# Another order of attention scores, gate blocks and transposes in a two-layer transformer mixer on one core

## The chip, the cores and the metric

The kernel runs on one core of one Trainium2 chip. The metric is the device time of one launch in microseconds (us); less is better. Before the change three runs gave 2495.41, 2496.18 and 2497.45 us, so the median is 2496.18 us.

## The reference, cut to what matters

The program computes a first block (a gated mixer of two branches and a mixture of 16 experts) and then a second block of two layers. Everything that is changed lies in the mixer of those two layers, `token_mixer_2`, on 256 tokens of width 1024:

```python
proj = u @ w_in                      # q 512, k 128, v 128, p 512, gates 2 x 1024
q, k = partial_rope(q), partial_rope(k)
scores = where(|qpos - kpos| <= 128, q @ k.T / 8, -1e30)      # 8 heads
probs = softmax(concat([scores, sink]))[..., :-1]
y_attn = (probs @ v) @ w_br_attn
y_pool = multiscale_pool(p) @ w_br_pool
out = (sigmoid(ga + b) * y_attn + sigmoid(gb + b) * y_pool) @ w_out
```

Each of the two layers is: half a feed-forward, this mixer, half a feed-forward, each on a normalized input and added to the stream.

## The kernel before, in words

Weights come as a stream of slots of 128x2048 fp32 values, 1 MB each, through a ring of 8 slots. SyncE reloads a slot when TensorE has signalled that it is used (`slot_used`, line 302). In the two layers every weight is taken apart into two fp32r numbers: ScalarE rounds a slot into `w_hi` (three buffers; `upper(n)`, line 499) and VectorE subtracts it from the slot in place (`lower(n)`, line 954). TensorE then makes three products for one (`product3`, line 1494). `upper(n)` waits until slot n-3 is used, for its buffer.

Each engine runs its own written list of steps and meets the others at semaphores alone. Nothing reorders the steps of ScalarE or VectorE: whatever stands at the head of the list holds back all behind it. The steps of one layer's mixer, with the names that matter here:

- **Gate blocks.** `gate(k)`, k from 0 to 7, is 48 matmuls on TensorE into bank 6 + k % 2 (line 1558); ScalarE's `gate(k)` waits for it, makes two sigmoids into `sgate` (line 551, tile mixer_area in the trace) and then does `upper` of the slot three further on (line 554). TensorE's gate(k) waits for ScalarE's gate(k-2), since they share a bank. TensorE's gate(k) also waits for VectorE's `lower` of slot 5 + k of the mixer.
- **Turned q and k.** Ten transposes (lines 1567 to 1571) into banks 0 to 2, copied out by ScalarE (lines 559 to 561, `qkT_kept`).
- **Scores.** `scores(t)` for the two halves of the queries, t = 0 and 1. TensorE makes eight small matmuls into banks 0 to 3. VectorE scales and masks them out of the banks (line 1020, `scores_kept`), takes the maximum (line 1024) and three small steps (`max_ready`). ScalarE's `exponentials(t)` makes eight exponentials with sums and one small one (lines 567 and 569, `att_exp`). VectorE's `probabilities(t)` scales by one over the sum (lines 1033 to 1035, `att_ready`). scores(1) on TensorE waits for `scores_kept` of half 0, since the banks are the same.
- **Transposes of probabilities.** `turn_att(c)`, c from 0 to 7, is four transposes; c from 0 to 3 is half 0, c from 4 to 7 half 1 (line 1582). Even c go to bank 4 and are copied by VectorE (line 1041), odd c go to bank 5 and are copied by ScalarE (line 574). turn_att(2) waits for VectorE's copy of 0, turn_att(3) for ScalarE's copy of 1.
- **Behind them.** Pooling matmuls (line 1608), mixed (line 1614), attention times v (line 1624), branch projections and the output projection.

The tiles have other names in the trace: `att` is area_h, `attT` is area_n, `sgate` and the maxima are mixer_area. TensorE's matmuls all have line 1101, its transposes line 1110.

The lists before, as far as they are touched. TensorE: gate 0, gate 1, turns of q and k, gate 2, scores 0, gate 3, gate 4, scores 1, turn_att 0, turn_att 1, gate 5, turn_att 2, turn_att 3, pooling, gate 6, mixed, gate 7, turn_att 4 to 7. ScalarE: gate 0, gate 1, copies of q and k, gate 2, exponentials 0, gate 3, gate 4, copy 1, exponentials 1, gate 5, copy 3, pooled copy, and so on. VectorE: lower 7, 8, 9, scores 0, lower 10, probabilities 0, lower 11, scores 1, lower 12, copy 0, copy 2, lower 13, probabilities 1, lower 14.

Of the kernel before, what the change touches and what calls it, by code (L numbers as in the profile page):

```python
# [25 lines left out]
TT = T // P  # L26
# [42 lines left out]
MIX_AT = 33  # L69
# [50 lines left out]
def build(nc, d):  # L120

    with ExitStack() as ctx:
# [5 lines left out]
        def sig(name):  # L128
            if name not in signals:
                signals[name] = ctx.enter_context(nc.semaphore(name))  # L130
            return signals[name]
# [44 lines left out]
        def bank(i):  # L176
            return ps[:, i, :]
# [4 lines left out]
        def lcol(name, i=0, n=1):  # L182
            return lcols[:, LCOLS[name] + i:LCOLS[name] + i + n]
# [128 lines left out]
        def _(act):  # L312
# [168 lines left out]
            with act.Fori(0, LAYERS) as l:  # L481
# [10 lines left out]
                def upper(n):  # L492

                    turn = l * (LAYER_SLOTS // RING) + (first + n) // RING
                    act.wait_ge(sig(f"slot_loaded{n % RING}"), turn * 16 + 16)
                    if n >= SPLITS:

                        act.wait_ge(sig("slot_used"), l * LAYER_SLOTS + first + n + 1 - SPLITS)
                    A.copy(w_hi[:, n % SPLITS, :], ring[:, n % RING, :]).then_inc(sig("w_hi_ready"), 1)  # L499
# [48 lines left out]
                def gate(k):  # L548
                    act.wait_ge(sig("gate_ps"), l * KD + k + 1)
                    for g in range(2):  # L550
                        last = A.activation(sgate[:, k, g, :], bank(6 + k % 2)[:, g * T:(g + 1) * T], ACT.Sigmoid,
                                            bias=lcol("b_gates", 8 * g + k))
                    last.then_inc(sig("gate_kept"), 1)
                    upper(MIX_AT + 8 + k)

                for k in range(2):
                    gate(k)
                act.wait_ge(sig("qkT_ps"), l + 1)
                A.copy(q2T[:, 0:2, :], bank(0).rearrange("p (j t) -> p j t", j=2))
                A.copy(q2T[:, 2:4, :], bank(1).rearrange("p (j t) -> p j t", j=2))  # L560
# [2 lines left out]
                def exponentials(t):  # L563

                    act.wait_ge(sig("max_ready"), l * TT + t + 1)
                    for h in range(8):
                        A.activation(att[:, t, h, :], att[:, t, h, :], ACT.Exp, bias=mst[:, t, 2, h:h + 1],  # L567
                                     accum_out=mst[:, t, 3, h:h + 1])
                    A.activation(mst[:, t, 1, :], mst[:, t, 1, :], ACT.Exp).then_inc(sig("att_exp"), 1)

                def keep_att(c):

                    act.wait_ge(sig("attT_ps"), l * 8 + c + 1)
                    A.copy(attT[:, (c // 2) % 2, (c % 2) * 4:(c % 2) * 4 + 4, (c // 4) * P:(c // 4 + 1) * P],
                           bank(4 + c % 2).rearrange("p (h q) -> p h q", h=4)).then_inc(sig("attT_kept_a"), 1)

                gate(2)
                exponentials(0)
                gate(3)
                gate(4)  # L580
                keep_att(1)
                exponentials(1)
                gate(5)
                keep_att(3)
                act.wait_ge(sig("pooled_ps"), l + 1)
                A.copy(pooledT, ps[:, 2:4, :].rearrange("p b (j t) -> p (b j) t", j=2)).then_inc(sig("pooled_kept"), 1)
                gate(6)
# [23 lines left out]
        def _(dve):  # L611
# [167 lines left out]
            for h in range(H):  # L779
# [28 lines left out]
                n = inter.rearrange("p t (s e) -> p t s e", s=2)[:, :, :, P]  # L808
# [136 lines left out]
            with dve.Fori(0, LAYERS) as l:  # L945
# [5 lines left out]
                def lower(n):  # L951

                    dve.wait_ge(sig("w_hi_ready"), l * SPLIT_SLOTS + n + 1)
                    V.tensor_tensor(ring_lo[:, n % RING, :], ring[:, n % RING, :], w_hi[:, n % SPLITS, :].bitcast(F32),  # L954
                                    ALU.subtract).then_inc(sig("w_ready"), 1)
# [59 lines left out]
                def scores(t):  # L1015

                    dve.wait_ge(sig("scores_ps"), l * TT + t + 1)
                    a = att[:, t, :, :]
                    m = mst[:, t, 0, :]
                    V.scalar_tensor_tensor(a, ps[:, 0:4, :].rearrange("p b (f k) -> p (b f) k", f=2), 0.125,  # L1020
                                           amask[:, t, :].unsqueeze(1).broadcast_to([P, 8, T]),
                                           ALU.mult, ALU.add).then_inc(sig("scores_kept"), 1)
                    dve.wait_ge(sig("scores_kept"), l * TT + t + 1)
                    step(V.tensor_reduce(m, a, X, ALU.max))  # L1024
                    step(V.tensor_tensor(m, m, lcol("sink", 0, 8), ALU.max))
                    V.tensor_tensor(mst[:, t, 1, :], lcol("sink", 0, 8), m, ALU.subtract)
                    V.tensor_scalar(mst[:, t, 2, :], m, -1.0, None, ALU.mult).then_inc(sig("max_ready"), 1)

                def probabilities(t):
                    dve.wait_ge(sig("att_exp"), l * TT + t + 1)  # L1030
                    a = att[:, t, :, :]
                    m = mst[:, t, 0, :]
                    step(V.tensor_tensor(m, mst[:, t, 3, :], mst[:, t, 1, :], ALU.add))
                    step(V.reciprocal(m, m))
                    V.tensor_tensor(a, a, m.unsqueeze(2).broadcast_to([P, 8, T]),
                                    ALU.mult).then_inc(sig("att_ready"), 1)

                def keep_att(c):

                    dve.wait_ge(sig("attT_ps"), l * 8 + c + 1)  # L1040
                    V.tensor_copy(attT[:, (c // 2) % 2, 0:4, (c // 4) * P:(c // 4 + 1) * P],
                                  bank(4).rearrange("p (h q) -> p h q", h=4)).then_inc(sig("attT_kept"), 1)

                for n in range(MIX_AT + 7, MIX_AT + 10):
                    lower(n)
                scores(0)
                lower(MIX_AT + 10)
                probabilities(0)
                lower(MIX_AT + 11)
                scores(1)  # L1050
                lower(MIX_AT + 12)
                keep_att(0)
                keep_att(2)
                lower(MIX_AT + 13)
                probabilities(1)
                lower(MIX_AT + 14)
                for g in range(4):
                    if g == 0:
# [35 lines left out]
        def _(pe):  # L1094
# [206 lines left out]
            for o in range(ORDERS):  # L1301
# [30 lines left out]
                for j in range(4):  # L1332
                    n = 0
# [90 lines left out]
            with pe.Fori(0, NE) as e:  # L1424
# [21 lines left out]
                for i in range(8):  # L1446
                    w = slot(2 * KD + i, turns)
                    for c in range(2):
                        for j in range(2):
                            k = 2 * i + j  # L1450
# [18 lines left out]
            with pe.Fori(0, LAYERS) as l:  # L1469
# [9 lines left out]
                def split(n):  # L1479

                    pe.wait_ge(sig("w_ready"), l * SPLIT_SLOTS + n + 1)
                    return w_hi[:, n % SPLITS, :], ring_lo[:, n % RING, :]
# [75 lines left out]
                def gate(k):  # L1558
                    if k >= 2:
                        pe.wait_ge(sig("gate_kept"), l * KD + k - 1)  # L1560
                    pair(split(MIX_AT + 5 + k), bank(6 + k % 2), sig("gate_ps"))

                for k in range(2):
                    gate(k)
                pe.wait_ge(sig("rope_ready"), l + 1)
                pe.wait_ge(sig("vp_kept"), l + 1)
                for j in range(5):
                    for t in range(TT):
                        turn(bank(j // 2)[:, (j % 2) * T + t * P:(j % 2) * T + (t + 1) * P],
                             qk[:, t, 2 * j:2 * j + 2, :].rearrange("p h c -> p (h c)"),  # L1570
                             ready=sig("qkT_ps") if j == 4 and t == 1 else None)
                gate(2)
                pe.wait_ge(sig("qkT_kept"), l + 1)

                def scores(t):
                    for j in range(4):
                        for f in range(2):

                            mm(bank(2 * f + j // 2)[:, (j % 2) * T:(j % 2 + 1) * T], q2T[64 * f:64 * f + 64, j, t * P:(t + 1) * P],
                               k2T[64 * f:64 * f + 64, :], ready=sig("scores_ps") if j == 3 and f == 1 else None)  # L1580

                def turn_att(c):

                    t, k, half = c // 4, (c // 2) % 2, c % 2
                    pe.wait_ge(sig("att_ready"), l * TT + t + 1)
                    if c >= 2:

                        pe.wait_ge(sig("attT_kept") if c % 2 == 0 else sig("attT_kept_a"), l * 4 + c // 2)
                    for i in range(4):
                        turn(bank(4 + c % 2)[:, i * P:(i + 1) * P], att[:, t, half * 4 + i, k * P:(k + 1) * P],  # L1590
                             ready=sig("attT_ps") if i == 3 else None)


                scores(0)
                gate(3)
                gate(4)
                pe.wait_ge(sig("scores_kept"), l * TT + 1)
                scores(1)
                turn_att(0)
                turn_att(1)  # L1600
                gate(5)
                turn_att(2)
                turn_att(3)

                pe.wait_ge(sig("scores_kept"), l * TT + 2)
                for g in range(4):
# [35 lines left out]
                for i in range(KD // 2):  # L1642
                    w = split(MIX_AT + 17 + i)
                    pe.wait_ge(sig("mT_ready"), l * KD + 2 * i + 2)
                    for t in range(TT):
                        for j in range(2):
                            k = 2 * i + j
# [176 lines left out]
```

## Time and profile before

| | |
|---|---|
| runs | 2495.41, 2496.18, 2497.45 us |
| profiled execution, its own time | 2499.19 us |
| span of its profile | 2497.3 us |
| TensorE busy | 2158.2 us (86%) |
| VectorE busy | 823.1 us (33%) |
| ScalarE busy | 597.7 us (24%) |
| granted TensorE clock, mean over the span | 0.919 |
| HBM read | 655.97 MB, 263 GB/s over the span |

The span is the time from the first to the last instruction in the profile; the run's own time is 1.9 us longer. The two layers take the last 1100 us of the span; the first layer's mixer begins near 1596 us, the second's near 2145 us. The granted clock is given as a share of 2.4 GHz: 1.00 is 2.4 GHz and 0.50 is 1.2 GHz. A stretch with a value between them holds a change from one to the other.

### The profile page before, as it was taken

How to read it: one execution, taken by the hardware profiler on the slowest of the kernel's cores; microseconds unless marked ns; L12 is line 12 of the kernel's file. 1: busy time of each engine (PE TensorE's matmuls, PEld its weight loads, DVE VectorE, ACT ScalarE, POOL GpSimd, SP SyncE). 2: the span in 40 equal slices, each digit the busy share in tenths (PEclk: the TensorE clock that was granted, in tenths of full speed). 3: DMA queues.
4: the chain of work that ended last, by engine and by line, in shares of the span. 5: the costliest groups of instructions: out<-in, count | busy, mean ns of one | idle time of the engine just before them, and what ended most of it. 6: DMA issues, size and time to landing. Idle time of an engine off the chain costs nothing.

```text
span 2497.3 us, 31333 instructions
## 1 busy us (share of the span) xinstructions
PE 2158.2 (86%) x12642; PEld 1440.0 (58%) x12642; DVE 823.1 (33%) x1079; ACT 597.7 (24%) x715; POOL 0.2 (0%) x4
## 2 busy tenths in 40 slices
PE   7999898777777777777777799998999999999998
PEld 2477674222222222222222699897999899888998
DVE  3422533000000000000000555556555555556554
ACT  2311101000000000000000433463433433463333
POOL 0000000000000000000000000000000000000000
PEclk9999998988788878888878899999999999999999
DMA  8336433999999999999999555433455455433552
GB/s 341 114 119 231 172 118 127 409 422 422 422 422 422 422 422 422 422 422 422 422 422 421 224 185 186 167 134 139 169 186 186 175 186 186 169 119 135 186 187 92
DMA packets 91395, 658.49 MB, mean 264 GB/s; under 512 B 10144, under 2 KB 10528, under 8 KB 11808
## 3 DMA queue, kind: packets, MB, share of 16 engines
q1 hardware_dynamic: 88992, 647.01, 65.8%
q10 hardware_dynamic: 2304, 10.05, 1.1%
q8 instruction: 76, 1.25, 0.2%
q14 instruction: 23, 0.19, 0.0%
HBM read 655.97 MB, written 1.05 MB: 263 GB/s over the span
## 4 chain that ended last, share of the span: by engine, by line
PE 62%; DMA 27%; DVE 5%; ACT 3%; issue 2%; SPq 0%; ACTq 0%; DVEq 0%
PE ps L1101 61%; DMA ring<-stream_dram 26%; PE ps L1110 1%; ACT w_hi L499 1%; ACT later L477 1%; DVE later L924 0%; DVE area_h L1020 0%; DVE mixer_area L1024 0%; DMA wide<-filt_dram 0%; DVE later L918 0%; DVE later L914 0%; DVE wide L788 0%; ACT area_h L567 0%; DVE wide L795 0%; DVE area_n L622 0%
## 5 line engine op out<-in xcount | busy, mean ns | idle before, releaser
L1101 PE MATMUL ps<-ring,later 128*32 128x512 f32 x3072 | 581.8, 750 | 208.4 <-DMA ring<-stream_dram 177.1
L1101 PEld LDWEIGHTS ps<-ring,later 128*32 128x32 f32 x3072 | 112.7, 124 | 648.0 <-DMA ring<-stream_dram 448.5
L954 DVE TENSOR_TENSOR ring_lo<-ring,w_hi 128x2048 fp32r<-128x2048 f32 x174 | 398.7, 2292 | 246.4 <-ACT w_hi L499 245.7
L1101 PE MATMUL ps<-u_hi,w_hi 128*128 128x256 f32 x1664 | 474.4, 285 | 2.9 <-DVE u_lo L961 2.9
L1101 PE MATMUL ps<-u_lo,w_hi 128*128 128x256 f32 x1664 | 473.0, 284 | 0.0
L1101 PE MATMUL ps<-u_hi,ring_lo 128*128 128x256 f32 x1664 | 472.1, 284 | 0.0
L499 ACT CAST w_hi<-ring 128x2048 fp32r<-128x2048 f32 x174 | 331.1, 1904 | 219.9 <-PE ps L1101 219.8
L1101 PEld LDWEIGHTS ps<-u_hi,w_hi 128*128 128x128 f32 x1664 | 318.8, 192 | 7.8 <-DVE u_lo L961 5.6
L1101 PEld LDWEIGHTS ps<-u_lo,w_hi 128*128 128x128 f32 x1664 | 317.6, 191 | 1.7
L1101 PEld LDWEIGHTS ps<-u_hi,ring_lo 128*128 128x128 f32 x1664 | 318.2, 191 | 0.0
L477 ACT COPY later<-ps 128x1024 f32<-128x1024 f32 x16 | 16.2, 1012 | 636.6 <-PE ps L1101 636.6
L924 DVE TENSOR_TENSOR later<-later,ps 128x512 f32<-128x512 f32 x16 | 11.0, 689 | 474.8 <-PE ps L1101 474.8
L1101 PE MATMUL ps<-area_h,ring 128*128 128x256 f32 (+1 forms) x640 | 153.4, 401 | 1.8 <-DVE wide L828 1.8
L1101 PEld LDWEIGHTS ps<-area_h,ring 128*128 128x128 f32 x640 | 121.4, 190 | 33.5 <-issue 17.1
L914 DVE TENSOR_TENSOR later<-ps,mod 128x256 f32<-128x256 f32 x16 | 6.8, 425 | 401.2 <-PE ps L1101 401.2
L1101 PE MATMUL ps<-w_hi,hid_lo 128*128 128x512 f32 x352 | 139.0, 395 | 0.0
L1101 PE MATMUL ps<-w_hi,hid_hi 128*128 128x512 f32 x352 | 138.5, 393 | 0.0
L1101 PE MATMUL ps<-ring_lo,hid_hi 128*128 128x512 f32 x352 | 138.0, 392 | 0.0
L524 ACT ACTIVATE area_n<-ps 128x256 f32<-128x256 f32 x88 | 33.8, 385 | 314.4 <-PE ps L1101 314.4
L1101 PE MATMUL ps<-wide 128*128 128x130 f32 (+5 forms) x244 | 73.6, 458 | 25.1 <-DMA wide<-filt_dram 8.7
L982 DVE TENSOR_TENSOR hid_hi<-ps,area_n 128x256 fp32r<-128x256 f32 x88 | 37.4, 425 | 154.7 <-ACT area_n L524 154.7
L1101 PE MATMUL ps<-later 128*128 128x512 f32 x144 | 68.3, 619 | 17.8 <-ACT later L477 17.8
(245 smaller groups left out, 1816.9 us busy)
## 6 DMA issues: line engine op xcount, KB each, us to landing
ring<-stream_dram SPq DMA_DIRECT2D x616, 1024.0 KB, 14.6
wide<-filt_dram ACTq DMA_DIRECT2D x1, 1728.0 KB, 7.5
wide<-tabs_dram ACTq DMA_DIRECT2D x1, 1408.0 KB, 10.4
tabs<-tabs_dram ACTq DMA_DIRECT2D x1, 1296.0 KB, 5.8
x_tok<-x_dram ACTq DMA_DIRECT2D x1, 1024.0 KB, 14.6
area_n<-ctx_dram ACTq DMA_DIRECT2D x1, 1024.0 KB, 19.1
fin_rows<-fin_rows_dram ACTq DMA_DIRECT2D x2, 512.0 KB, 4.2
out_dram<-x_tok SPq DMA_DIRECT2D x2, 512.0 KB, 2.6
```

What stands on the lines that cost most here:

```text
L477: A.copy(ye, ps[:, 6:8, :].rearrange("p b n -> p (b n)")).then_inc(sig("ye_ready"), 1)
L499: A.copy(w_hi[:, n % SPLITS, :], ring[:, n % RING, :]).then_inc(sig("w_hi_ready"), 1)
L524: A.activation(sa2[:, i % 2, :], bank(4 + i % 4)[:, 0:T], ACT.Silu).then_inc(sig("silu2_ready"), 1)
L914: V.tensor_tensor(xe, bank(5)[:, 0:KD * CAP].rearrange("p (k c) -> p k c", k=KD), mod2[:, :].unsqueeze(2).broadcast_to([P, KD, CAP]), ALU. ...
L924: V.tensor_tensor(hid_e, sa, bank(5), ALU.mult).then_inc(sig("hid_e_ready"), 1)
L954: V.tensor_tensor(ring_lo[:, n % RING, :], ring[:, n % RING, :], w_hi[:, n % SPLITS, :].bitcast(F32), ALU.subtract).then_inc(sig("w_ready" ...
L982: V.tensor_tensor(hid_hi[:, i % 4, :], b, sa2[:, i % 2, :], ALU.mult)
L1101: ins = M.matmul(out, lhsT, rhs, start=start, stop=stop, **more)
L1110: ins = M.transpose(out, src, ident[0:rows, 0:rows])
```

## The change

It only moves steps within the written lists of ScalarE, VectorE and TensorE, in the body of the loop over the two layers. No instruction is added or taken away, and no semaphore's meaning changes. After it, TensorE's list is: gate 0, turns of q and k, gate 1, scores 0, gate 2, scores 1, gate 3, gate 4, turn_att 0 to 3, gate 5, pooling, gate 6, mixed, gate 7, turn_att 4 to 7. ScalarE's is: gate 0, copies of q and k, gate 1, exponentials 0, gate 2, gate 3, exponentials 1, gate 4, copy 1, copy 3, gate 5, pooled copy. VectorE's is: lower 7, 8, scores 0, lower 9, scores 1, probabilities 0, lower 10, 11, copy 0, copy 2, probabilities 1, lower 12, 13, 14.

```diff
--- before.py
+++ after.py
@@ -553,8 +553,7 @@
                     last.then_inc(sig("gate_kept"), 1)
                     upper(MIX_AT + 8 + k)
 
-                for k in range(2):
-                    gate(k)
+                gate(0)
                 act.wait_ge(sig("qkT_ps"), l + 1)
                 A.copy(q2T[:, 0:2, :], bank(0).rearrange("p (j t) -> p j t", j=2))
                 A.copy(q2T[:, 2:4, :], bank(1).rearrange("p (j t) -> p j t", j=2))
@@ -574,14 +573,15 @@
                     A.copy(attT[:, (c // 2) % 2, (c % 2) * 4:(c % 2) * 4 + 4, (c // 4) * P:(c // 4 + 1) * P],
                            bank(4 + c % 2).rearrange("p (h q) -> p h q", h=4)).then_inc(sig("attT_kept_a"), 1)
 
+                gate(1)
+                exponentials(0)
                 gate(2)
-                exponentials(0)
                 gate(3)
+                exponentials(1)
                 gate(4)
                 keep_att(1)
-                exponentials(1)
+                keep_att(3)
                 gate(5)
-                keep_att(3)
                 act.wait_ge(sig("pooled_ps"), l + 1)
                 A.copy(pooledT, ps[:, 2:4, :].rearrange("p b (j t) -> p (b j) t", j=2)).then_inc(sig("pooled_kept"), 1)
                 gate(6)
@@ -1041,18 +1041,19 @@
                     V.tensor_copy(attT[:, (c // 2) % 2, 0:4, (c // 4) * P:(c // 4 + 1) * P],
                                   bank(4).rearrange("p (h q) -> p h q", h=4)).then_inc(sig("attT_kept"), 1)
 
-                for n in range(MIX_AT + 7, MIX_AT + 10):
+                for n in range(MIX_AT + 7, MIX_AT + 9):
                     lower(n)
                 scores(0)
+                lower(MIX_AT + 9)
+                scores(1)
+                probabilities(0)
                 lower(MIX_AT + 10)
-                probabilities(0)
                 lower(MIX_AT + 11)
-                scores(1)
-                lower(MIX_AT + 12)
                 keep_att(0)
                 keep_att(2)
+                probabilities(1)
+                lower(MIX_AT + 12)
                 lower(MIX_AT + 13)
-                probabilities(1)
                 lower(MIX_AT + 14)
                 for g in range(4):
                     if g == 0:
@@ -1560,8 +1561,7 @@
                         pe.wait_ge(sig("gate_kept"), l * KD + k - 1)
                     pair(split(MIX_AT + 5 + k), bank(6 + k % 2), sig("gate_ps"))
 
-                for k in range(2):
-                    gate(k)
+                gate(0)
                 pe.wait_ge(sig("rope_ready"), l + 1)
                 pe.wait_ge(sig("vp_kept"), l + 1)
                 for j in range(5):
@@ -1569,7 +1569,7 @@
                         turn(bank(j // 2)[:, (j % 2) * T + t * P:(j % 2) * T + (t + 1) * P],
                              qk[:, t, 2 * j:2 * j + 2, :].rearrange("p h c -> p (h c)"),
                              ready=sig("qkT_ps") if j == 4 and t == 1 else None)
-                gate(2)
+                gate(1)
                 pe.wait_ge(sig("qkT_kept"), l + 1)
 
                 def scores(t):
@@ -1592,15 +1592,14 @@
 
 
                 scores(0)
+                gate(2)
+                pe.wait_ge(sig("scores_kept"), l * TT + 1)
+                scores(1)
                 gate(3)
                 gate(4)
-                pe.wait_ge(sig("scores_kept"), l * TT + 1)
-                scores(1)
-                turn_att(0)
-                turn_att(1)
+                for c in range(4):
+                    turn_att(c)
                 gate(5)
-                turn_att(2)
-                turn_att(3)
 
                 pe.wait_ge(sig("scores_kept"), l * TT + 2)
                 for g in range(4):
```

## Rows read from the trace of the kernel before

**Rows 1.** The page's chain that ended last, by engine, shares of the span.
```profile
PE 62%; DMA 27%; DVE 5%; ACT 3%; issue 2%; SPq 0%; ACTq 0%; DVEq 0%
```

**Rows 2.** Waits in the first layer's mixer, TensorE and DMA queue: total, times, longest.
```profile
PE ps L1110 <- DVE area_n L1041: 3.5, 2, 3.2
PE ps L1110 <- ACT area_n L574: 1.4, 1, 1.4
...
SPq L303 <- PE ps L1101: 67.4, 9, 14.7
```

**Rows 3.** Timeline of TensorE, first layer's mixer: start, length, instruction, [idle before].
```profile
1624.59 0.28 PE L1101 MATMUL ps<-u_hi,w_hi 128*128 128x256 f32 x1
...
1636.02 1.26 PE L1110 MATMUL ps<-const,hid_area 128*128 128x128 f32 x10
...
1637.03 0.36 PE L1101 MATMUL ps<-u_hi,w_hi 128*128 128x256 f32 x1
...
1642.92 2.00 PE L1101 MATMUL ps<-mixer_area 64*128 64x256 f32 x16
...
1644.85 0.39 PE L1101 MATMUL ps<-u_hi,w_hi 128*128 128x256 f32 x1
...
1656.48 2.00 PE L1101 MATMUL ps<-mixer_area 64*128 64x256 f32 x16
...
1658.41 1.09 PE L1110 MATMUL ps<-const,area_h 128*128 128x128 f32 x8
...
1668.37 1.97 PE L1110 MATMUL ps<-const,area_h 128*128 128x128 f32 x8 [3.16 <-DVE area_n L1041]
```

**Rows 4.** Timeline of ScalarE, the same stretch.
```profile
1643.03 0.84 ACT L551 ACTIVATE mixer_area<-ps,lcols 128x256 f32<-128x256 f32 x2 [2.93 <-PE ps L1101]
...
1643.75 1.90 ACT L499 CAST w_hi<-ring 128x2048 fp32r<-128x2048 f32 x1
...
1645.67 1.28 ACT L567 ACT_TABLE_LOAD   x1
...
1650.09 0.51 ACT L567 ACTIVATE area_h<-area_h,mixer_area 128x256 f32<-128x256 f32 x1 [3.14 <-DVE mixer_area L1027]
...
1658.80 1.92 ACT L499 CAST w_hi<-ring 128x2048 fp32r<-128x2048 f32 x1
...
1660.60 0.61 ACT L574 COPY area_n<-ps 128x512 f32<-128x512 f32 x1
```

**Rows 5.** Timeline of VectorE, the same stretch.
```profile
1644.96 2.29 DVE L1020 SCALAR_TENSOR_TENSOR area_h<-ps,tabs 128x2048 f32<-128x2048 f32 x1 [3.79 <-PE ps L1101]
...
1649.97 2.28 DVE L954 TENSOR_TENSOR ring_lo<-ring,w_hi 128x2048 fp32r<-128x2048 f32 x1
...
1654.28 0.17 DVE L1033 TENSOR_TENSOR mixer_area<-mixer_area 128x8 f32<-128x8 f32 x1 [2.03 <-ACT mixer_area L569]
...
1654.72 2.29 DVE L1035 TENSOR_TENSOR area_h<-area_h,mixer_area 128x2048 f32<-128x2048 f32 x1
...
1667.63 0.69 DVE L1041 COPY area_n<-ps 128x512 f32<-128x512 f32 x1
```

**Rows 6.** Busy us (x) of PE, PEld, DVE, ACT, POOL; PEclk; DMA share; GB/s.
```profile
1668.37:1670.34 1.97, 1.97 (x9) 1.97 (x10) 0.69 (x1) 1.95 (x8) 0.00 (x0) 0.50 0.30 33
...
1670.34:1675.47 5.13, 5.13 (x16) 4.13 (x16) 1.81 (x1) 3.77 (x5) 0.00 (x0) 0.61 0.47 192
...
2217.19:2219.16 1.97, 1.97 (x9) 1.97 (x10) 0.69 (x1) 1.95 (x8) 0.00 (x0) 0.50 0.31 42
...
2219.16:2222.97 3.81, 3.81 (x18) 3.24 (x16) 0.48 (x1) 3.77 (x5) 0.00 (x0) 0.83 0.61 254
...
2241.16:2246.36 5.20, 5.20 (x32) 3.47 (x33) 0.30 (x1) 0.00 (x0) 0.00 (x0) 0.69 0.01 3
```

**Rows 7.** Timeline of TensorE's turns ahead of the first mixer.
```profile
1592.62 3.50 PE L1110 MATMUL ps<-const,area_n 128*128 128x128 f32 x16 [2.63 <-DVE area_n L622]
```

**Rows 8.** Stretch at the end of those turns, columns as in rows 6.
```profile
1595.00:1596.00 1.00, 1.00 (x7) 0.88 (x5) 0.08 (x1) 0.95 (x3) 0.00 (x0) 0.59 0.89 369
```

## The prediction

> **What bounds the kernel now.** I read the page's chain first: TensorE carries 62% of it and the DMA of weights 27% [rows 1]. The DMA share lies in the first block and the experts. In the two layers the DMA queue waits for TensorE to free slots, 67.4 us in nine waits within one mixer [rows 2], so loads are not what a new order there can help or harm. Then I read TensorE's waits in one mixer [rows 2]. Of all its idle time the one large piece is 3.2 us before turn_att(2), ended by VectorE's copy of turn_att(0). The second layer's answer has the same rows. Then the timelines of the three engines over the same stretch [rows 3 to 5]: from 1624.59 on TensorE goes without a gap through gates, turns and scores until gate 5 ends, stands until 1668.37, and goes on. The last view is the granted clock in stretches [rows 6]: after this stall it is at 0.50, that is 1.2 GHz, and what follows runs slowly.
>
> So an order of steps can be worth three things per layer: the 3.2 us stall, the slow running behind it, and any new stall. TensorE's own work is the same before and after, since nothing is added.
>
> **What VectorE was doing in the stall.** Its copy of turn_att(0) stands behind scores(1) and lower 12 and starts at 1667.63 [rows 5]; the transposes for it had been made at about 1659. The change moves scores(1) forward by two gates, so that this copy no longer waits for it. That part does what it says. But turn_att(3) waits for the other copy, ScalarE's, and ScalarE's list has changed too: exponentials(1) and gate 4 now stand before it.
>
> **The working, first layer.** Lengths from the rows: a gate block takes (1636.02 - 1624.59) / 2 = 5.71 us, or (1656.48 - 1644.85) / 2 = 5.82 us behind small work; ten turns 1.01 us (1637.03 - 1636.02); scores 1.93 us (1644.85 - 1642.92) [rows 3].
>
> TensorE after: gate 0 from 1624.59, turns of q and k at 1630.30, gate 1 at 1631.31, scores(0) one gate earlier than now, at 1642.92 - 5.71 = 1637.21, gate 2 at 1639.14, scores(1) at 1644.96, gate 3 at 1646.89, gate 4 at 1652.71. Gate 4 ends at 1658.41, as the same five gates, turns and both scores do now [rows 3].
>
> Do the waits on this way hold it? The turns of q and k end at 1631.3; until scores(0) at 1637.2 ScalarE has one cast (1.9 us) and three copies (0.6 us each, by the copy of the same width) to do, 3.7 us [rows 4]: no wait. VectorE reads scores(0) at 1644.96 - 5.71 = 1639.25 and is done 2.29 later, at 1641.6 [rows 5]; scores(1) wants the banks at 1644.96: no wait, 3.4 us to spare. The maxima are there 5.13 us after that reading starts (1644.96 to 1650.09) [rows 4, 5], so exponentials(0) starts at 1644.38 and lasts 4.19 us (1650.09 to 1654.28), to 1648.57. Then ScalarE loads its table (1.28 us [rows 4]) and makes gate 2's sigmoids, done by 1650.7. Gate 4 wants that bank at 1652.71: no wait, with 2.0 us to spare. VectorE does lower 9 (2.29 us [rows 5]) in between, then scores(1) from 1647.0 to 1652.1, probabilities(0) in 2.73 us (1654.28 to 1654.72 + 2.29) [rows 5] to 1654.8, lower 10 and 11 until 1659.2, and copies turn_att(0) until 1659.9. TensorE made turn_att(0) and (1) by 1659.5, so it waits **0.4 us** for turn_att(2), in place of 3.2.
>
> Now turn_att(3). ScalarE starts gate 3's sigmoids 0.11 us behind TensorE's end of that block [rows 3, 4], at 1652.8. Sigmoids to cast 0.72 us, cast to table load 1.92 us [rows 4]: the table for exponentials(1) is loaded from 1655.5 to 1656.8, 4.7 us after the maxima of half 1 are ready at 1652.1. Exponentials(1) then take 4.19 us, to 1660.9. Gate 4's table load and sigmoids: 1.28 + 0.72, to 1662.9. Its cast: 1.80 us (1658.80 to 1660.60) [rows 4], to 1664.7. The copy of turn_att(1): 0.61 us [rows 4], to 1665.3. Handing over to TensorE takes 0.05 us (1667.63 + 0.69 against 1668.37) [rows 3, 5]. TensorE has ended turn_att(2) at 1660.5 and waits for turn_att(3) until 1665.4: **4.9 us**. Queued behind it are gate 5 and all that follows.
>
> Stalls: 5.3 us in place of 3.2 us, plus 0.1 us because four transposes alone don't overlap those behind them: +2.2 us a layer. Both layers have the same timing, so **+4.5 us**. What else moved costs nothing: lower 12 ends near 1667.2 and gate 7 wants it after 1680, under cover of gates 5 and 6; if that cover went, its 2.29 us would show. The waits behind gate 7 (1.4 us for ScalarE's copy of turn_att(5) [rows 2], and smaller ones) stay, as their lists are unchanged. Bounds of the stall term: VectorE's and ScalarE's parts could each be off by one small operation, some 0.3 us; ends +1.6 and +2.8 us a layer.
>
> **The clock.** Behind the stall the first layer ran eight turns at 0.50 and pooling at 0.61: 1.97 x 0.50 + 5.13 x 0.39 = 3.0 us lost. The second ran them at 0.50 and 0.83: 1.0 + 3.81 x 0.17 = 1.6 us lost; 4.6 in all [rows 6]. With a longer stall the clock is surely low when TensorE resumes, and gate 5 takes the place of turns and pooling as the work that runs slowly. I bound each layer by these two rows, 1.6 and 3.0, and take their mean, 4.6 for both layers. The same program also lost 5.20 x 0.31 = 1.6 us in the second layer behind gate 7 and not in the first [rows 6], so this part varies by itself.
>
> The profiled execution took 2499.19 us, 3.0 above the median. That is just what lies between it and an execution with two short slow stretches (3.2 in place of 4.6 us) and none behind gate 7 (1.6). Against the median the clock term of the change is then between 0 and +1.4; I take +0.6. Sum: 2499.19 + 4.5 for the profiled execution at equal clock, and **2496.18 + 4.5 + 0.6 = 2501.3 us** for the median.
>
> **A rule against the rows.** Eight turns at 0.50 come first behind the stall now; after the change only four, then a block of real matmuls. Ahead of the first mixer sixteen turns alone took 3.50 us [rows 7], and the clock was back near their end (0.59 in a stretch that ends at 1.00, or 1595.8) [rows 8]. The Trainium skill, TensorE: Matmul & The Clock Gate, section Part 4: PE-mode transpose, says that transposes don't count as work that brings the full clock back. The trace disagrees there, as turns alone brought it back. By the page the new order should always give the short stretch: the rival below gives its time from rows.
>
> **Rivals.**
> - The clock returns early in both layers, since matmuls follow the stall almost at once: 1.6 us lost in each, 3.2 in place of 4.6. For: the second layer's 0.83 [rows 6]. Against: rows 7 and 8, and the first layer's stretch with the same instructions. Time: 2496.18 + 4.5 - 1.4 = 2499.3. Chance 0.25; within 0.2%.
> - The clock stays low for the long stretch in both layers: 3.0 each, 6.0 in place of 3.2 for a median execution. 2496.18 + 4.5 + 2.8 = 2503.5. For: the longer stall. Chance 0.22; slower.
> - Faster: turn_att(3) finds its copy made and both stalls vanish, the clock stays up. 2 x 3.2 + 4.6 = 11.0 us less, 2485.2. It decides at ScalarE's start of copy 1, which would have to be by about 1660, while I have exponentials(1) ending at 1660.9 and 3.8 us of gate 4 before the copy. Half of it (exponentials(1) starting at 1652.1) would still give a faster kernel. For: VectorE's chain did get shorter. Against: ScalarE's written order. Chance 0.08.
>
> **How the numbers follow.** My forecast has 0.45 and lies at 2499.9 to 2502.7, on both sides of 0.2% (5.0 us, about what a measurement of this kernel can tell from no change): 0.26 of it above, 0.19 below. Slower: 0.26 + 0.22 = 0.48. Same: 0.19 + 0.25 = 0.44. Faster: 0.08. The range leaves out the faster case: low end 2496.18 + 3.2 - 1.4 = 2498.0 (stall at its lower bound, short slow stretches), high end 2496.18 + 5.6 + 2.8 = 2504.6.
>
> **What would show it.** Right: in both layers a wait of TensorE for area_n of line 574 of 4 to 6 us before a group of four transposes, a wait for line 1041 under 1 us, and PEclk 0.50 at the start of gate 5. exponentials(1) start right behind a table load, not behind a wait for VectorE. Wrong: no wait above 1 us before gate 5; or a new wait before gate 4 or scores(1); or a gain behind gate 7.

## The result and the profile after

The changed kernel takes 2502.89 us in the median of 10 runs (2501.49 to 2506.62), the kernel before 2495.57 us in 10 runs (2494.17 to 2498.33). The ratio is 1.0031, 95% interval 1.0023 to 1.0040: slower by 7.3 us. The forecast was 2501.3 us, with a range of 2498.0 to 2504.6.

The profiled execution of the changed kernel took 2502.87 us at a span of 2501.0 us. The waits of TensorE over both mixers, total, times and longest; line 573 is ScalarE's copy of a turned block, 1041 VectorE's, and TensorE's transposes are now line 1111:

```profile
PE ps L1111 <- DVE area_n L622: 15.5, 7, 4.8
PE ps L1111 <- ACT area_n L573: 13.0, 4, 5.1
...
PE ps L1111 <- DVE area_n L1041: 1.4, 4, 0.3
```

The wait that stood before, 3.2 us for VectorE's copy [rows 2], has shrunk to 0.35 us. In its place is one of 5.1 us for ScalarE's copy, in both layers. The timeline of TensorE in the first layer's mixer shows where:

```profile
1629.79 1.25 PE L1111 MATMUL ps<-const,hid_area 128*128 128x128 f32 x10
...
1636.69 2.00 PE L1102 MATMUL ps<-mixer_area 64*128 64x256 f32 x16
...
1644.52 2.00 PE L1102 MATMUL ps<-mixer_area 64*128 64x256 f32 x16
...
1657.99 1.03 PE L1111 MATMUL ps<-const,area_h 128*128 128x128 f32 x8
1659.37 0.66 PE L1111 MATMUL ps<-const,area_h 128*128 128x128 f32 x4 [0.35 <-DVE area_n L1041]
1665.13 1.09 PE L1111 MATMUL ps<-const,area_h 128*128 128x128 f32 x4 [5.10 <-ACT area_n L573]
```

From the turns of q and k to turn_att(1) nothing waits; the scores of half 1 come 12 us earlier than before (1644.52 against 1656.48 [rows 3]). Then turn_att(3) stands for 5.10 us. ScalarE's timeline says what it did meanwhile:

```profile
1655.12 1.28 ACT L566 ACT_TABLE_LOAD   x1
1656.41 0.51 ACT L566 ACTIVATE area_h<-area_h,mixer_area 128x256 f32<-128x256 f32 x1
...
1660.58 1.28 ACT L551 ACT_TABLE_LOAD   x1
1661.87 0.84 ACT L551 ACTIVATE mixer_area<-ps,lcols 128x256 f32<-128x256 f32 x2
1662.60 1.90 ACT L499 CAST w_hi<-ring 128x2048 fp32r<-128x2048 f32 x1
1664.39 0.59 ACT L573 COPY area_n<-ps 128x512 f32<-128x512 f32 x1
```

Exponentials 1, a table load, gate 4's sigmoids and its cast run one behind another, and the copy comes last. The maxima of half 1 were ready at 1651.6, but exponentials 1 could only start at 1656.41, so the earlier scores brought nothing here: ScalarE was the engine with the queue.

The granted clock (PEclk is the third number from the end) from turn_att(3) to the end of gate 5 in both layers, and through attention times v in the first:

```profile
1665.13:1673.86 8.73, 8.73 (x53) 8.73 (x54) 1.69 (x1) 0.59 (x1) 0.00 (x0) 0.68 0.00 0
2217.61:2225.04 7.43, 7.43 (x52) 7.43 (x53) 1.70 (x1) 0.59 (x1) 0.00 (x0) 0.82 0.00 0
1695.32:1700.32 5.00, 5.00 (x33) 3.36 (x33) 0.30 (x1) 0.00 (x0) 0.00 (x0) 0.72 0.02 3
```

Lost behind the two waits: 8.73 x 0.32 + 7.43 x 0.18 = 4.1 us, and 1.4 us behind gate 7. The profiled execution before lost 4.6 and 1.6 us in these places [rows 6]. So between the two profiled executions the clock in these places counts for -0.7 us, and the stalls for +4.6 us (2 x (0.35 + 5.10 - 3.16)); 3.9 us together, and the two executions lie 3.7 us apart. The medians lie 7.3 us apart, of which the stalls explain 4.6. What the other 2.7 us are is the question that one pair of profiles can't answer.

### The profile page after: what moved, and what is told of

The parts are those of the page before. It is cut to its first block, busy times and chain, and to the rows that moved or that the text cites. A ratio compares the mean times of both kernels' runs of the same rounds, so it can differ in the third digit from the quotient of the medians.

```text
span 2501.0 us, 31333 instructions
## 1 busy us (share of the span) xinstructions
PE 2159.9 (86%) x12642; PEld 1437.9 (57%) x12642; DVE 822.7 (33%) x1079; ACT 598.1 (24%) x715; POOL 0.2 (0%) x4
## 4 chain that ended last, share of the span: by engine, by line
PE 63%; DMA 27%; DVE 5%; ACT 3%; issue 2%; SPq 0%; ACTq 0%; DVEq 0%
PE ps L1102 62%; DMA ring<-stream_dram 26%; PE ps L1111 1%; ACT w_hi L499 1%; ACT later L477 1%; DVE later L924 0%; DMA wide<-filt_dram 0%; DVE later L918 0%; DVE later L914 0%; ACT area_h L566 0%; DVE wide L788 0%; DVE wide L795 0%; DVE area_n L622 0%; ACT area_n L333 0%; ACT wide L433 0%
```

## The experiments

My theory: the stall sits in ScalarE's list, ahead of its copy of turn_att(1), and the rest is the clock. Each ratio below is against runs of the kernel before on the same chip.

**The copy ahead of gate 4.** In ScalarE's list:

```diff
                 exponentials(1)
+                keep_att(1)
                 gate(4)
-                keep_att(1)
                 keep_att(3)
```

> The changed kernel with ScalarE's copy of turn_att(1) put ahead of its gate 4 instead of behind it. My theory (the changed kernel waits 5.1 us per layer for this copy because ScalarE's list has exponentials 1 and gate 4 ahead of it, and the clock falls in that wait): the copy starts behind exponentials 1 near 1660.6 in place of 1664.4, the wait for line 573 shrinks from 5.1 to about 1.3 us in both layers, 7.7 us less, and where the clock stays at 1.00 another 3 to 5 us less: 2490 to 2492 us, some 4 to 5 us under the kernel before. Rival (another thing ends the wait, such as a weight slot or VectorE): the wait stays near 5 us and the time within 2 us of 2502.9.

Measured: 2490.84 us, ratio 0.9979 (0.9969 to 0.9989). TensorE's timeline and the granted clock from turn_att(3) to the end of gate 5 in the first layer:

```profile
1660.06 0.63 PE L1111 MATMUL ps<-const,area_h 128*128 128x128 f32 x4 [1.14 <-ACT area_n L573]
```

```profile
1660.06:1666.24 6.18, 6.18 (x52) 6.18 (x53) 4.51 (x2) 4.27 (x5) 0.00 (x0) 1.00 0.22 91
```

One step moved ahead of one other takes the wait from 5.10 to 1.14 us (1.15 in the second layer), and the clock stays at 1.00 in both layers. The whole gain is 12.0 us, of which 7.9 are the waits. The rival falls.

**Gate 5 back between the transposes.** On TensorE; ScalarE's copy 3 goes behind gate 5 to match:

```diff
-                for c in range(4):
+                for c in range(2):
                     turn_att(c)
                 gate(5)
+                for c in range(2, 4):
+                    turn_att(c)
```

> The changed kernel with gate 5 put back between turn_att(1) and turn_att(2) on TensorE (and between copies 1 and 3 on ScalarE); the new order of scores stays. My theory: gate 5 covers both waits, since copy 1 is made at about 1665.0 and gate 5 ends at 1664.9; no wait over 0.4 us ahead of pooling, 10.9 us less than the changed kernel, and with the clock at 1.00 through the gates another 3 to 5 us: 2487 to 2489 us. Rival (the new order of scores itself costs time, on whichever engine): a new wait of some us elsewhere before gate 6, and a time at or above the kernel before, 2495.6.

Measured: 2485.48 us, ratio 0.9961 (0.9947 to 0.9975), 17.4 us under the changed kernel and 10.6 us under the runs of the kernel before. Timeline and waits of TensorE in the first layer's mixer:

```profile
1657.09 1.04 PE L1111 MATMUL ps<-const,area_h 128*128 128x128 f32 x8
1663.68 1.19 PE L1111 MATMUL ps<-const,area_h 128*128 128x128 f32 x8
```

```profile
PE ps L1111 <- ACT area_n L573: 1.4, 1, 1.4
...
PE ps L1111 <- DVE area_n L1041: 0.3, 1, 0.3
```

No wait is left before pooling; the rows that remain belong behind gate 7. The time is even 1.5 us under what I had written. So the change has two parts of opposite sign. Scores of both halves early, which this version keeps, is a gain of 10.6 us: 6.3 us are the two old waits, and that the other 4.3 us are the clock is argued and not shown. The transposes put together ahead of gate 5 cost 17.4 us. The sum is a loss of 6.8 us, against 7.3 measured.

**The wait filled with matmuls.** To part the clock from the stall, the changed kernel does 40 extra matmuls in its long wait. They read `u_hi` and write bank 0, which is free there. In the run's kernel they stand in a small helper; here, and in the other fillings, they are written out in place:

```diff
-                for c in range(4):
+                for c in range(3):
                     turn_att(c)
+                for i in range(40):
+                    mm(bank(0)[:, 0:T], u_hi[:, i % 8, 0:P], u_hi[:, i % 8, :])
+                turn_att(3)
                 gate(5)
```

> The changed kernel with 40 extra matmuls of 0.12 us, whose product nothing reads, put into TensorE's wait before turn_att(3): the wait's length stays, but the clock has no idle stretch to fall in. If the part of the loss beyond the stalls (7.3 us measured less 4.6 of longer stalls) is the clock: the granted clock is 1.00 through gate 5, and the time is 4 to 5 us less than the changed kernel, about 2498 us. Rival (the clock is not part of it): within 1 us of 2502.9, or above by what the filling overruns.

Measured: 2493.54 us (12 runs, 2490.48 to 2503.19), ratio 0.9991 (0.9979 to 1.0003). That is 9.4 us less with more work, not 4 to 5. The granted clock from the filling to the end of gate 5 in the first layer:

```profile
1657.16:1668.69 11.53, 11.21 (x95) 11.04 (x94) 5.55 (x5) 5.76 (x11) 0.00 (x0) 1.00 0.21 85
```

So the clock behind the wait is part of the loss, and the rival falls. But the gain is over twice the 4.1 us that the changed kernel's profile lost there.

**The same for the kernel before**, with 24 matmuls ahead of turn_att(2), into bank 6 behind a wait for gate 4's sigmoids:

```diff
                 gate(5)
+                pe.wait_ge(sig("gate_kept"), l * KD + 5)
+                for i in range(24):
+                    mm(bank(6)[:, 0:T], u_hi[:, i % 8, 0:P], u_hi[:, i % 8, :])
                 turn_att(2)
```

> The kernel before with 24 extra matmuls of 0.12 us, whose product nothing reads, put into TensorE's 3.2 us wait before turn_att(2). The clock stays at 1.00 through turns and pooling. If the kernel before lost less to the clock than the changed one in the median (my reading: 2 to 3 us in place of 4 to 6), this gains only 2 to 3 us, to about 2493 us, and the difference of the two filled kernels is that of the stalls alone, 4.6 us. Rival (both lose the same to the clock): this gains 4 to 5 us, to 2491, and the filled kernels differ by 7 us.

Measured: 2491.74 us, ratio 0.9983 (0.9974 to 0.9992), 4.3 us under the runs of the kernel before. That is the gain that I wrote for the rival (4 to 5), not that of my reading (2 to 3). The granted clock is 1.00 behind the filled wait:

```profile
1672.22:1676.77 4.55, 4.54 (x26) 4.13 (x27) 0.69 (x1) 4.52 (x11) 0.00 (x0) 1.00 0.28 117
```

The second half of the expectation fails for both: the two filled kernels differ by 1.8 us, where my reading had the 4.6 us of the stalls and the rival 7. Their intervals overlap, but 1.8 us says that filling gave the changed kernel more than the clock behind its two waits, or that scatter of some 2 us is left in these medians (the same filled kernel comes out 2.1 us higher below).

**The changed kernel again, filled and not, on one chip.**

> The changed kernel, unaltered, once more on the chip of the two that follow, so that they can be compared without a change of chip. My theory: 2502 to 2504 us again, two waits for line 573 of 5.1 us, and the granted clock at 0.50 behind each, for 3 to 6 us of busy time.

> The first filled version of the changed kernel once more (40 matmuls whose product nothing reads in the 5.1 us wait). It came out 9.4 us under the changed kernel, more than the 4.3 us that its profile shows lost behind the two waits. Theory A (the clock term is near 6 us in the median and the rest was scatter): 2495 to 2497 us, 6 to 8 us under the unaltered one. Theory B (filling gives more than the clock): 2493 to 2494 again, 9 to 10 us under.

Measured: 2503.57 us without (7 runs, 2501.47 to 2504.26; ratio 1.0028, 1.0017 to 1.0039), 2495.67 us filled (11 runs, 2492.49 to 2503.09; ratio 1.0004, 0.9995 to 1.0013): 7.9 us. Time and difference are those of theory A, the difference at its upper end. The granted clock in the profile of the unfilled one, from turn_att(3) to the end of gate 5 and through attention times v, in each layer:

```profile
1665.15:1673.88 8.73, 8.73 (x52) 8.73 (x53) 1.70 (x1) 0.59 (x1) 0.00 (x0) 0.67 0.00 0
1695.34:1700.40 5.06, 5.06 (x33) 3.43 (x33) 0.30 (x1) 0.00 (x0) 0.00 (x0) 0.72 0.02 3
2217.90:2227.00 9.10, 9.10 (x54) 9.07 (x55) 1.69 (x1) 0.66 (x2) 0.00 (x0) 0.68 0.00 0
2248.19:2253.30 5.11, 5.11 (x33) 3.44 (x33) 0.30 (x1) 0.00 (x0) 0.00 (x0) 0.71 0.01 3
```

and of the filled one, from the filling to the end of gate 5:

```profile
1658.62:1670.15 11.53, 11.21 (x96) 11.03 (x94) 5.55 (x5) 5.76 (x11) 0.00 (x0) 1.00 0.21 85
2205.14:2216.68 11.54, 11.22 (x95) 11.05 (x94) 5.55 (x5) 5.77 (x11) 0.00 (x0) 1.00 0.22 87
```

The same program as in the first profile after lost 2.9 us behind each wait here (8.73 x 0.33, 9.10 x 0.32), and 1.4 and 1.5 us behind gate 7. The filled one lost nothing in these places.

But the two profiled spans, 2501.8 and 2492.4 us, differ by more than their mixers do. From the first transposes of a mixer to those of the feed-forward behind it the filled execution is 3.8 us shorter in the first layer (1592.15 to 1750.84 against 1590.80 to 1745.70) and 2.3 us in the second (2144.88 to 2303.61 against 2135.78 to 2292.24). That is 6.1 us of the 9.4; the other 3.3 us lie where not one instruction differs. One such place is the start of the feed-forward behind the first mixer, where TensorE waits 2.3 to 2.4 us for its input in every version. The clock in the ten microseconds behind that wait, for the kernel before, the same filled, the changed kernel and the same filled:

```profile
1747.95:1757.95 10.00, 9.06 (x50) 8.43 (x51) 6.44 (x11) 6.49 (x13) 0.00 (x0) 0.66 0.27 105
1750.55:1760.55 10.00, 8.44 (x66) 7.93 (x67) 6.44 (x11) 6.52 (x14) 0.00 (x0) 1.00 0.30 107
1750.84:1760.84 10.00, 8.92 (x50) 8.28 (x51) 6.43 (x11) 6.45 (x12) 0.00 (x0) 0.66 0.27 105
1745.70:1755.70 10.00, 8.49 (x67) 7.97 (x68) 6.44 (x11) 6.53 (x13) 0.00 (x0) 1.00 0.27 107
```

The clock falls here in both unfilled kernels and in neither filled one. Over all ten profiles it falls at the start of the feed-forward behind the mixer in 10 of 20 layers. So the 7.9 us are the whole effect of the filling and not only the clock behind the two waits, and whether the fall here goes by what the mixer did or by chance is not shown.

**The wait filled with transposes.**

```diff
-                for c in range(4):
+                for c in range(3):
                     turn_att(c)
+                for i in range(54):
+                    turn(bank(0)[:, 0:P], ident)
+                turn_att(3)
                 gate(5)
```

> The changed kernel with 54 transposes of 0.09 us, whose product nothing reads, in the 5.1 us wait, in place of matmuls. If transposes keep the clock up as matmuls do (as turns alone brought it back near 1595.8 us in the kernel before): PEclk 1.00 through the filling and gate 5, and the time of the version filled with matmuls, 2494 to 2497 us. Rival (the Trainium skill, TensorE: Matmul & The Clock Gate, section Part 4: PE-mode transpose, by which transposes do not count as work): PEclk falls to 0.50 within the filling or at gate 5, and the time is that of the unaltered kernel, 2502 to 2504 us or more, since the filling itself then runs over the wait.

Measured: 2497.35 us (11 runs), ratio 1.0008 (0.9999 to 1.0017). The timeline of the filling, and the clock from it to the end of gate 5 in both layers:

```profile
1659.15 6.06 PE L1111 MATMUL ps<-const 128*128 128x128 f32 x54
1665.04 0.60 PE L1111 MATMUL ps<-const,area_h 128*128 128x128 f32 x4
```

```profile
1659.15:1671.20 12.05, 12.05 (x109) 12.05 (x108) 5.55 (x5) 5.68 (x11) 0.00 (x0) 1.00 0.20 82
2208.33:2220.38 12.05, 12.05 (x109) 12.05 (x108) 5.55 (x5) 5.68 (x11) 0.00 (x0) 1.00 0.21 83
```

Six microseconds of nothing but transposes hold the clock at 1.00. They took 0.11 us each and not 0.09, so the filling runs over the wait by some 0.6 us a layer. This version lies 1.7 us above the one filled with matmuls, 1.3 us of it by that; a difference of this size is within the scatter of the filled versions. It also lies 0.4 us above the 2494 to 2497 us that I had written. The rival, the rule of the Trainium skill, falls in this kernel.

**A version that beats both.** The version with gate 5 between, and ScalarE's cast behind gate 7 moved behind its copies 5 and 7:

```diff
                     last.then_inc(sig("gate_kept"), 1)
-                    upper(MIX_AT + 8 + k)
+                    if k < 7:
+                        upper(MIX_AT + 8 + k)
...
                 keep_att(7)
+                upper(MIX_AT + 15)
```

> The version with gate 5 back between turn_att(1) and turn_att(2), and also ScalarE's cast behind gate 7 moved behind its copies of turn_att(5) and (7). Theory: the wait of 1.4 us for copy 5 goes, as the copy no longer stands behind a cast of 1.9 us; the one of 0.8 us ahead of attention times v stays; 1.4 us less a layer, 2.8 us, and less often a low clock behind gate 7: 2481 to 2483 us against 2485.5. Rival (the cast, now later, is missed by VectorE's lower 15 and the branch blocks behind it): a new wait behind mixed products and no gain.

Measured: 2477.81 us (5 runs, 2476.29 to 2480.53), ratio 0.9929 (0.9916 to 0.9943). That is 17.7 us or 0.7% under the kernel before, and 7.7 us under the version without the second edit, where I had expected 2.5 to 4.5. TensorE behind gate 7 in the first layer, and the clock there:

```profile
1683.11 1.04 PE L1113 MATMUL ps<-const,area_h 128*128 128x128 f32 x8
1684.49 1.09 PE L1113 MATMUL ps<-const,area_h 128*128 128x128 f32 x8 [0.35 <-DVE area_n L1043]
1686.35 3.70 PE L1104 MATMUL ps<-area_n,vbias 128*64 128x256 f32 x32 [0.77 <-ACT area_n L574]
```

```profile
1683.11:1690.00 6.89, 5.78 (x51) 4.43 (x49) 3.34 (x3) 3.81 (x5) 0.00 (x0) 1.00 0.46 155
```

The wait of 1.42 us is gone in both layers (2.8 us), and the clock does not fall. In the version without this edit it did, through attention times v in the first layer:

```profile
1686.17:1691.50 5.33, 5.33 (x33) 3.63 (x33) 0.30 (x1) 0.00 (x0) 0.00 (x0) 0.68 0.01 3
```

5.33 x 0.32 = 1.7 us, and 1.6 us in the second layer. With 2.8 us that makes 6.1 of the 7.7, as far as one profile of each can say. The rest is within the scatter of 5 and 8 runs. The cast that now comes later is not missed: VectorE waits longer for casts (17.5 us in place of 10.7 between 1680 and 1745 us), but TensorE has no new wait behind it, so the rival falls.

## Why the prediction was right, and where its size was off

- **TensorE's way to gate 4.** Right to 0.1 us in every length. The changed kernel's profile stands 0.4 to 0.5 us ahead of my times all the way (turns of q and k 1629.79 against 1630.30, first scores 1636.69 against 1637.21, second 1644.52 against 1644.96), so only its start differs. None of the waits that I checked for shows up: not the copies of q and k, not the banks of the scores, not gate 2's sigmoids.
- **turn_att(2).** Predicted wait 0.4 us, measured 0.35, in place of 3.2.
- **turn_att(3).** Predicted 4.9 us by ScalarE's list, measured 5.10 in both layers. Exponentials 1 start behind a table load, as forecast.
- **The stall term.** Predicted +4.5 us, measured 4.6.
- **The clock term.** This is the one that was mis-sized. I set +0.6, between 0 and +1.4. The stalls leave 2.7 us of the measured loss (7.3 less 4.6), and some 3.5 us by the second measurement of the changed kernel (2503.57 against 2495.52 us of the kernel before, less 4.6). In the profiles the clock behind the stalls and behind gate 7 lost 6.2 us before, and 5.5 and 8.7 us in the changed kernel, so -0.7 and +2.5 us.
- Part of that is a slip in the working. The mean of the two rows, 4.6 us, less the 3.2 us that I gave a median execution of the kernel before, is +1.4 and not +0.6, and the two rows bound the term by 0 and +2.8. With +1.4 the forecast would have been 2502.1. The 3.2 us themselves were a guess: filling the kernel before gains 4.3 us in the median. In the faster rival I took off 4.6 us in place of these 3.2, so its time should read 2486.6.
- The filled versions don't size the term either. Filling gains 7.9 to 9.4 us in the changed kernel and 4.3 us in the one before, 3.6 to 5 us more, but part of it lies far from the waits, and the filled kernels differ by 1.8 us (3.9 with the second measurement), not by the 4.6 us of the stalls.
- Where the clock term failed in substance: I bounded a layer's loss by the two rows behind the old stall, 1.6 and 3.0 us, and took their mean for the new one. The long stretch is what the changed kernel got in three of four layers profiled (2.8, 1.3, 2.9, 2.9 us), and the fall behind gate 7, which I left as unchanged scatter, was in three of those four as well.
- **The rivals.** The early return of the clock in both layers is out by the runs. The long stretch in both layers, 2503.5 us and chance 0.22, is the nearest of all my cases to the median, which lies just above the 2499.9 to 2502.7 us of my main case. That the measured time lies in the stated range is the stall term's merit; that the sum is off by no more than 1.6 us is in part luck, since the clock behind the same stalls lost 4.1 us in one profile and 5.8 in the other. The faster case failed where I had put its point: the copy started at 1664.4 and not by 1660. The first experiment shows that only gate 4 stood in the way for most of it.

What stays open is why the clock falls behind gate 7 in some executions and not in others with the same waits there (0.35, 1.42 and 0.77 us; it fell in 11 of 18 layers), and the same for the start of the feed-forward. Neither profile of the changed kernel filled with matmuls has the fall behind gate 7; the kernel before, filled, has it in both layers. So filling may have helped further on or it may be chance; no run here tells these apart.

## What to carry to other kernels

When steps are moved forward on one engine, follow each result through the written list of every engine that must still touch it: here the scores came 12 us earlier, and what decided was a 0.6 us copy that stood behind 8 us of other work on ScalarE. Put small copies that another engine waits for ahead of casts and sigmoids that nobody needs yet, and keep a block of independent matmuls between transposes and those that wait for their copies. A stall of TensorE of 3 to 5 us should be priced with the slow running behind it: here 1.6 and 3.0 us behind the 3.2 us stalls, and 1.3 to 2.9 us behind the 5.1 us ones. Part of that price varies from one execution to the next, so take it from several profiles of the kernel before and from medians.

## What was not expected of the hardware

A stall costs more than its length: behind the two 5.1 us waits the changed kernel loses another 4.1 to 5.8 us by slow running, and giving TensorE useless matmuls in the same wait makes the whole kernel 7.9 us faster. Useless transposes do nearly the same, 6.2 us: the granted clock is 1.00 through 6.06 us of 54 transposes and the gate behind them. The Trainium skill, TensorE: Matmul & The Clock Gate, section Part 4: PE-mode transpose, says that transposes don't count as activity for the clock; the trace disagrees, both here and by [rows 7, 8]. The trace lists these transposes as fp32 matmuls with a constant tile and doesn't show whether they run in the mode that the page means.

No long wait is needed for a fall. Waits of 0.35 and 1.14 us left the clock at 1.00 in both layers of the one profile that has them, while three waits of 0.35, 1.42 and 0.77 us with only transposes between them saw it fall to 0.50 in 11 of 18 layers. That it is their sum that counts, and not chance, is not shown.
